# A two-block transformer step on one core: opening blocks merged, a layer norm folded into the next products, gates and last norm in parts, key choice in more steps

## What is computed

```python
# sparse attention: which keys each query may see
idx_s = relu(einsum('bqhd,bsd->bqhs', qib, ki))          # 8 index heads
idx_s = einsum('bqh,bqhs->bqs', wib, idx_s)
_, sel = top_k(where(causal, idx_s, -inf), 64)
# differential attention
lam = exp(sum(lp[0] * lp[1])) - exp(sum(lp[2] * lp[3])) + lam_init
# end of the first block, start of the second
x = rms_norm(x, final_norm_g)
h = x; hn = rmsnorm(h, attn_norm[0]); proj = hn @ w_in
# end of each layer
e = rmsnorm(p[i] @ ple_w_proj[i], ple_norm[i])
gate = sigmoid(rmsnorm(h, ple_gate_norm[i]) @ ple_w_gate[i])
h = h + gate * e
# end
return rmsnorm(h, final_norm)
```

## Time and profile before

| | |
|---|---|
| median of 3 runs | 2309.53 us (2305.46 to 2318.35) |
| the profiled execution | 2314.81 us, of which the span from first to last instruction 2313.0 |
| busy: TensorE / its weight loads | 1997.3 us (86%) / 1917.7 us (83%) |
| busy: DVE / ACT | 1529.7 us (66%) / 1222.2 us (53%) |
| granted TensorE clock, mean | 0.928 of full |
| HBM read | 293.26 MB, 127 GB/s over the span |

### The profile page before, as it was taken

The page is one execution under the profiler, slowest core; times in us unless marked ns, Lnnn a source line. Parts: engine busy times, 40 slices in busy tenths (PEclk is TensorE's granted clock), DMA queues, the critical chain, the costliest instruction groups (busy, mean ns, idle before and its releaser), DMA issues. The chain is left out here.

```text
span 2313.0 us, 44158 instructions
## 1 busy us (share of the span) xinstructions
PE 1997.3 (86%) x15796; PEld 1917.7 (83%) x15796; DVE 1529.7 (66%) x3122; ACT 1222.2 (53%) x2396; POOL 15.3 (1%) x21
## 2 busy tenths in 40 slices
PE   6998888999999766999999873896998968799895
PEld 5887778999999756999998863796998957799895
DVE  4657555999644688666665657765687567568755
ACT  4454554777755698555555453102555543555553
POOL 0000000000000000000000000000000001000000
PEclk9999998999999899999999996886999989799998
DMA  4422333445555301555554430001455523045441
GB/s 169 146 100 92 121 99 119 157 171 187 175 190 183 98 0 36 191 193 193 194 191 163 140 107 19 1 1 46 160 193 164 173 73 128 10 159 192 164 165 55
DMA packets 95216, 295.97 MB, mean 128 GB/s; under 512 B 9203, under 2 KB 25718, under 8 KB 94582
## 3 DMA queue, kind: packets, MB, share of 16 engines
q1 hardware_dynamic: 95094, 294.35, 37.9%
HBM read 293.26 MB, written 1.05 MB: 127 GB/s over the span
## 5 line engine op out<-in xcount | busy, mean ns | idle before, releaser
L381 PE MATMUL bank<-a_high,w_high 128*128 128x256 f32 x3256 | 937.9, 288 | 132.2 <-DVE a_low L741 61.9
L355 DVE TENSOR_TENSOR w_low<-ring,w_high 128x512 fp32r<-128x512 f32 x1102 | 747.3, 689 | 429.3 <-ACT w_high L349 424.5
L349 ACT ACTIVATE w_high<-ring 128x512 fp32r<-128x512 f32 x1102 | 680.0, 628 | 463.6 <-PE bank L383 459.6
L382 PE MATMUL bank<-a_low,w_high 128*128 128x256 f32 x3256 | 922.4, 283 | 0.0
L383 PE MATMUL bank<-a_high,w_low 128*128 128x256 f32 x3256 | 921.8, 283 | 0.0
L381 PEld LDWEIGHTS bank<-a_high,w_high 128*128 128x128 f32 x3256 | 632.9, 194 | 150.2 <-issue 107.1
L382 PEld LDWEIGHTS bank<-a_low,w_high 128*128 128x128 f32 x3256 | 629.4, 193 | 0.4
L383 PEld LDWEIGHTS bank<-a_high,w_low 128*128 128x128 f32 x3256 | 629.7, 193 | 0.0
L381 PE MATMUL bank<-s_high,w_high 128*128 128x256 f32 x1024 | 282.7, 276 | 2.0 <-DVE s_low L1872 2.0
L383 PE MATMUL bank<-s_high,w_low 128*128 128x256 f32 x1024 | 282.6, 276 | 0.0
L382 PE MATMUL bank<-s_low,w_high 128*128 128x256 f32 x1024 | 282.6, 276 | 0.0
(11 more groups left out here) (309 smaller groups left out, 2033.4 us busy)
## 6 DMA issues: line engine op xcount, KB each, us to landing
ring<-in_stream SPq DMA_DIRECT2D x279, 512.0 KB, 3.6
ring<-in_peer_u SPq DMA_DIRECT2D x128, 512.0 KB, 3.5
ring<-in_peer_v SPq DMA_DIRECT2D x128, 512.0 KB, 3.4
ring<-in_stream SPq DMA_DIRECT2D x32, 256.0 KB, 3.2
consts<-in_consts SPq DMA_DIRECT2D x1, 1024.0 KB
x<-in_x SPq DMA_DIRECT2D x1, 1024.0 KB, 7.1
arena<-in_mem SPq DMA_DIRECT2D x1, 1024.0 KB, 9.1
out<-x SPq DMA_DIRECT2D x1, 1024.0 KB, 4.0
```

What stands on the lines that cost most here:

```text
L349: self.nc.scalar.activation(self.w_high[:, h % SLOTS, :], self.raw(h), ACT.Copy)\
L355: self.nc.vector.tensor_tensor(self.w_low[:, h % SLOTS, :], self.raw(h), self.w_high[:, h % SLOTS, :].bitcast(F32), ALU.subtract)\
L381: self.nc.tensor.matmul(to, lh, rh, start=start, stop=False, **more)
L382: self.nc.tensor.matmul(to, lh, rl, start=False, stop=False, **more)
```

## The change

Five edits. (1) `load` issues lambda's row, six of the sixteen constants, x in four parts with a semaphore each, two weight groups, the other constants, two weight groups and the memory input, 14 DMAs, and waits for positions, params, lambda and the six constants; input copies and squares wait for their part of x. `lambda_of` is gone; its work is in `rope_tables`, with Exp ahead of Sin on ACT. (2) `choose_steps` scores two index heads a step in steps 0 to 7, with one Relu for both, and DVE does two multiply-adds a step; the maxima of a round come in an even step from 10 on, its replacements in the odd step after. (3) `between` is gone. The hybrid products take x times both gains (their product is made in `rope_tables`); with s the mean square of x and t the mean square of gained x, the root is over (s + eps) times (t/(s + eps) + eps). Squares of gained x go to an unused place, their sums to bank 6, and `whole` writes x times the first gain and root. (4) In `ple` the second block is gone; scaling e (`embed`), sigmoid and multiply-add (`apply`, by halves of a unit) are duties. (5) `finish` is one block with squares, gains on ACT, products and stores by pairs of chunks, and a small Sqrt first, which loads the table.

```diff
     def products(...)
+        if applied(len(units) - 1):
+            duties += [(units[norms[1][2]].end + 4, 4, "embed", c) for c in range(DC)]
...
-                    duties.append((max(end(u, h) + late, soon), 3, "unit", (u, h)))
+                    key = max(end(u, h) + late, soon)
+                    duties.append((key, 3, "unit", (u, h)))
+                    if applied(u):
+                        key = max(key, units[norms[1][2]].end + 4)
+                        duties += [(key + 1, 4, "sigmoid", (u, h)), (key + 2, 4, "apply", (u, h))]
...
# TensorE, sums of squares
+                            for c in range(norm.chunks if isinstance(norm, Twice) else 0):
+                                nc.tensor.matmul(self.bank[6][:, 0:T], self.const("ones"),
+                                                 norm.squares[:, c, :], start=c == 0,
+                                                 stop=c == norm.chunks - 1)
...
# ACT, squares and root
+                        if isinstance(norm, Twice):
+                            for c in range(norm.chunks):
+                                nc.scalar.activation(norm.squares[:, c, :], norm.source[:, c, :],
+                                                     ACT.Square, scale=self.param(norm.first, c))
...
+                        if isinstance(norms[what][0], Twice):
+                            nc.scalar.activation(inverse[1], inverse[1], ACT.Sqrt)
...
# DVE, root
+                        if isinstance(norms[what][0], Twice):
+                            link(nc.vector.tensor_scalar(inverse[1], summed[what], 1.0 / D, EPS,
+                                                         ALU.mult, ALU.add))
+                            link(nc.vector.reciprocal(inverse[1], inverse[1]))
+                            link(nc.vector.scalar_tensor_tensor(
+                                out=inverse[0], in0=self.bank[6][:, 0:T], scalar=1.0 / D,
+                                in1=inverse[1], op0=ALU.mult, op1=ALU.mult))
+                            link(nc.vector.tensor_scalar(inverse[0], inverse[0], EPS, None, ALU.add))
+                            link(nc.vector.reciprocal(inverse[0], inverse[0]))
+                            nc.vector.tensor_tensor(inverse[0], inverse[0], inverse[1], ALU.mult)\
+                                .then_inc(mean.up(), 1)
...
# DVE, the gates
+                    elif kind == "apply":
+                        u, h = what
+                        n = units[u].tile + 2 * h
+                        place, to = units[u].place, half(u, h)[1]
...
+                        link(nc.vector.tensor_tensor(to, to, place.by[:, n:n + 2, :], ALU.mult))
+                        nc.vector.tensor_tensor(place.to[:, n:n + 2, :], place.to[:, n:n + 2, :], to,
+                                                ALU.add)
...
     def load
-                for to, n in ((self.params[:, :], "params"), (self.consts[:, :, :], "consts")):
-                    sp.dma_start(to, self.dram[n]).then_inc(loaded.up(16), 16)
-                sp.dma_start(self.x[:, :, :], self.dram["x"]).then_inc(self.x_landed.up(16), 16)
+                sp.dma_start(self.consts[:, 0:soon, :], self.dram["consts"][:, 0:soon, :])\
+                    .then_inc(loaded.up(16), 16)
+                for c in range(4):
+                    sp.dma_start(self.x[:, 2 * c:2 * c + 2, :], self.dram["x"][:, 2 * c:2 * c + 2, :])\
+                        .then_inc(self.x_landed[c], 16)
...
     def choose_steps
-                if 18 <= i < 18 + N_SEL // 8:
+                if i in range(10, 10 + 2 * (N_SEL // 8), 2):
                     for b in range(TT):
                         ins = nc.vector.max(out=best[:, 8 * b:8 * b + 8], in_=total(b))
                     link(ins)
+                if i in range(11, 11 + 2 * (N_SEL // 8), 2):
                     for b in range(TT):
                         ins = nc.vector.match_replace(out=total(b), in_to_replace=best[:, 8 * b:8 * b + 8],
                                                       in_values=total(b), imm_value=TAKEN)
...
     def hybrid
-        h = Normed(x, "attn_norm_2.0")
+        h = Twice(x, "final_norm_g", "attn_norm_2.0", place(8))
+        free[0] -= 8 * T
...
     def finish
+                nc.scalar.activation(self.small[:, T:T + 1], self.const("ones")[:, 0:1], ACT.Sqrt)
+                for c in range(0, DC, 2):
+                    nc.scalar.activation(hn[:, c:c + 2, :], x[:, c:c + 2, :], ACT.Square)\
+                        .then_inc(squares.up(), 1)
...
+                for c in range(0, DC, 2):
+                    dve.wait_ge(gained.sem, gained.at(c + 2))
+                    nc.vector.tensor_tensor(x[:, c:c + 2, :], x[:, c:c + 2, :], inverse.unsqueeze(1)
+                                            .broadcast_to([P, 2, T]), ALU.mult).then_inc(ready.up(), 1)
...
+                for c in range(0, DC, 2):
+                    sp.wait_ge(ready.sem, ready.at(c // 2 + 1))
+                    sp.dma_start(self.out[:, c:c + 2, :], x[:, c:c + 2, :]).then_inc(stored.up(16), 16)
```

More of the change, by code:

```diff
@@ L136, with __init__ @@
 class Normed:
-    def __init__(self, source, gain, chunks=DC, size=D):
+    def __init__(self, source, gain, chunks=DC, size=D, ready=()):
         self.source, self.gain, self.chunks, self.size = source, gain, chunks, size
+        self.ready = ready
+class Twice(Normed):
+    def __init__(self, source, first, both, squares):
+        super().__init__(source, both)
+        self.first, self.squares = first, squares
 class Times:
@@ L921, in rope_tables @@
         MAGIC = 1.5 * 2.0 ** 23
+        dots, weights, exps = (self.counter(s) for s in ("lambda_dots", "lambda_spread", "lambda_exps"))
+        if lam is not None:
+            lambdas = self.at(70 * T, 1, 256)[0:1, 0, :]
+            prod = self.at(70 * T + 256, 1, 256)[0:1, 0, :]
+            dot = self.at(70 * T + 512, 1, 16)[0:1, 0, :]
         two_pi = 2 * math.pi
@@ L964, in _ @@
                                  start=True, stop=True).then_inc(spread.up(), 1)
+                if lam is not None:
+                    pe.wait_ge(dots.sem, dots.at(1))
+                    nc.tensor.matmul(self.bank[1][:, 0:2], self.consts[0:1, CONST_AT["ones"], :],
+                                     dot[:, 0:2], start=True, stop=True).then_inc(weights.up(), 1)
             @block.scalar
             def _(act):
+                if lam is not None:
+                    act.wait_ge(weights.sem, weights.at(1))
+                    nc.scalar.activation(lam[:, 1:3], self.bank[1][:, 0:2], ACT.Exp)\
+                        .then_inc(exps.up(), 1)
                 act.wait_ge(angles.sem, angles.at(1))
@@ L1349, in choose_steps @@
         count = 27
[L1350 to L1351 removed]
+        pairs = [(0, 2), (4, 6), (1, 3), (5, 7)] * 2
+        keys = lambda f: (f // 4 + 1) * P
+        part = lambda f: idx[:, 2 + 2 * (f % 2):4 + 2 * (f % 2), 0:keys(f)]
+        scores = lambda f: self.bank[bank][:, 0:2 * keys(f)].rearrange("p (h s) -> p h s", h=2)
         total = lambda b: idx[:, b, 0:(b + 1) * P]
@@ L1896, in expert_sum @@
         self.taken += N_KEYS * BLK
-    def between(self):
-        x = self.x
-        self.norm(lambda c: x[:, c, :], lambda c: self.param("final_norm_g", c),
-                  lambda c: x[:, c, :])
     def ffn(self, l):
@@ L1924, in ple @@
                        (f"ple_gate.{l}", "fm", Normed(x, f"ple_gate_norm_2.{l}"),
[L1925 to L1943 removed]
+                        Applied(lambda n, c: gate[:, n:n + c, :], e, f"ple_norm_2.{l}", x))],
+                      also=Normed(e, f"ple_norm_2.{l}"), after=(self.fetched, self.fetched.total))
     def mla(self):
@@ L2578, in finish @@
         nc = self.nc
-        x = self.x
-        self.norm(lambda c: x[:, c, :], lambda c: self.param("final_norm_2", c),
-                  lambda c: x[:, c, :])
-        stored = self.counter("stored")
-        with nc.Block(no_gpsimd_drain=True) as block:
+        x, hn = self.x, self.hn
+        squares, sums, mean, root, gained, ready, stored = (
+            self.counter(s) for s in ("squares_ready", "square_sums_ready", "mean_ready", "root_ready",
+                                     "gained", "output_ready", "stored"))
```

218 lines of the change are left out of this document (122 added, 96 removed).

## The result

The changed kernel takes 2294.61 us (median of 7 runs, 2289.82 to 2300.44), the kernel before in the same comparison 2312.89 (2300.59 to 2318.35): a ratio of 0.9927, 95% interval 0.9900 to 0.9953. That is 18.3 us less, and within 1.4 us of the forecast of 2293.2. The profiled execution of after has a span of 2298.5 us (it took 2300.44) at a mean granted clock of 0.926; before, 2313.0 at 0.928.

The account below looks back on a forecast made before the run. TensorE, busy 86%, bounds the kernel, so other engines' work matters only where it stands still. Start -3.0, choice -4.3, hybrid -4.8, gates -3.1 and end -1.1 sum to -16.3 us: 2293.2 us, range 2280 to 2305.

Parts of the forecast that it names:

- The start: Kernel start: lambda block removed, -3.7, against longer DMA issuing, net +0.7; sum -3.0 us, bounds -4 and -1.
- Rival 4: Kernel start: slow issues and a late exponent leave no gain there; total -13.3 us, 2296.2; chance 0.1.
- The key choice: Key choice: rounds spread over steps 10 to 25 take 5.7 us off DVE's late steps; -4.3, bounds -6 and 0.
- the deduction of 1.4 us: Key choice: 1.4 of the 5.7 us falls where DVE waits for TensorE's mixed values and a high weight part.
- rival 5: Key choice: paired scores make TensorE wait for ACT's Relu; at 3.6 us a step +12.5, 2322; chance 0.04.
- The hybrid: Hybrid products: folding in the final norm removes a block but lengthens the root; -4.8 us, bounds -8 and 0.
- three terms: Hybrid products: earlier start -11.5 us, eight more matmuls with ones +3.3, longer root chain on DVE and ACT +3.4.
- rival 2: Hybrid root and gates: new TensorE waits lower its clock, 10.8 us lost over three places; total -5.5, 2304; chance 0.12.
- The gates: Embedding gates: DVE work mostly changes places; layer 0 -0.5, layer 1 -2.6, sum -3.1 us, bounds -6 and +2.
- The end: Last norm and stores: 17.5 us after x is complete against 18.66; -1.1 us, bounds -3 and +1.5.
- Rival 3: Kernel end: ACT's table switch also drains, costing 1.4 us more; total -14.9, 2294.6; chance 0.06.
- Rival 1: DVE already full where work goes: gates 0, choice 2, hybrid start 3; total -8 us, 2301.5; chance 0.2.

Follow-up runs that it names:

- `only_choice`: The kernel before with the new key choice alone: 2302.08 us against 2309.96, ratio 0.9954.
- `only_hybrid`: The kernel before with the final norm folded into the hybrid products alone: 2307.82 us, ratio 1.0010 to before.
- `after_again`: The changed kernel, unedited, run and profiled a second time: 2294.48 us against 2313.53 before, ratio 0.9923.
- `one_sum`: The changed kernel without the hybrid norm's eight gained sums, second reciprocal and its small operations; trace only: shift against before -16.14 us at cut 690.
- `later_again`: The changed kernel with every norm's root two half-groups later, in a second comparison: 2279.17 us, ratio 0.9847 to before.
- `scale_one`: The changed kernel without seven of the eight embedding scalings in each gate; trace only: gates give -3.6 and -5.2 us against before.
- `only_ends`: The kernel before with the merged first blocks and the new `finish` alone: 2305.48 us, ratio 0.9978 to before.
- `old_root_later`: The kernel before with only every norm's root two half-groups later: 2291.20 us, ratio 0.9925 to before.
- `root_later`: The changed kernel with every norm's root two half-groups later, first comparison: 2267.12 us against 2304.87, ratio 0.9843.
- `both_later`: The changed kernel with every norm's root two half-groups later and the gained squares spread over weight cuts: 2275.74 us, ratio 0.9857 to before.
- `squares_spread`: The changed kernel with the eight gained squares spread over the first unit's weight cuts; trace only: hybrid stage gives -5.35 us to cut 690.

## Why the prediction was right

**The start: right at -3.0, with two sizes off.** The load block ended 1.25 us later, not 0.7. The wait of 1.4 us for constants went whole, as reckoned; the issues took longer, and end at 7.80, not 7.35: 2.64 us later than before. The first product gained only 2.5; the other 0.5 came by cut 10. Rival 4 (nothing at the start) falls.

**The key choice: mechanism right, size too small.** The step that failed is the deduction of 1.4 us: I took DVE's load in steps 18 to 25 as 5.7 less and said that 1.4 of it fell where DVE waits for TensorE's mixed values at 176. Alone it gives 6.5, all of the 5.7 and 0.8 more. The operation that takes the mixed values, before and in `only_choice`:

```profile
176.03 0.23 DVE L1114 TENSOR_SCALAR arena<-arena 128x4 f32<-128x4 f32 x1 [0.88 <-PE bank L1060]
```

```profile
174.19 0.23 DVE L1114 TENSOR_SCALAR arena<-arena 128x4 f32<-128x4 f32 x1 [1.68 <-PE bank L1060]
```

DVE's wait grows by 0.8 us, not 1.4, and the values do not stay at 176: against cut 50 they come 1.5 us earlier. Behind them stood seven of the eight rounds, now three pairs of maxima and four of replacements, 3.5 rounds or 5.0 us less. 1.5 + 5.0 = 6.5. What brings the mixed values forward was not tried by itself. The steps that took the moved work (scores from 125 to 168 us before) did not take it at no cost all along: in `only_choice` the shift against cut 50 is +3.7 at cut 62, and 0 again at cut 67. As it comes back within the stage, the forecast holds, and rival 5 (paired scores that wait) falls.

The clock is not what the choice gains by. In `only_hybrid`, with the old choice, it was at 1.00 from 165 to 206 us, TensorE waited 11.0 us for low weights instead of 8.5, and cuts 50 to 78 took only 0.25 us less than before; and the new choice gives 6.3 in `after_again` at 1.00, and 6.5 in after at 0.83. In all of them DVE's queue sets the end of the stage. Behind it the clock does count. In the first trace of after 0.8 us of the choice's gain were lost again by cut 82, with a fall at 193.4 us (0.83 on 190 to 200), and 1.5 more with a fall at 220.7 us (0.86 on 217 to 229); `after_again`, with 1.00 on both, lost nothing.

**The hybrid: three terms right, one missing.** -11.5 was -11.6, +3.3 and +3.4 were together +6.8 (of which `one_sum` gives back 6.0). Missing was the clock: behind the wait of 4.6 us it falls to 1.2 GHz, and the next half-groups lose 1.4 (after) to 2.8 us (`only_hybrid`). The windows behind the root, first after, then `after_again`:

```profile
1285.00:1292.00 7.00, 5.90 (x39) 5.90 (x40) 5.91 (x11) 3.19 (x7) 0.00 (x0) 0.76 0.47 150
```

```profile
1285.00:1295.00 10.00, 8.76 (x53) 8.76 (x54) 7.68 (x14) 4.15 (x8) 0.00 (x0) 0.66 0.37 123
```

So rival 2 came true in one of its three places, at under its size for one (3.6). In the gates the clock fell too, in one of the two traces each (layer 0: 0.83 on 1852 to 1862 in after, 1.00 in `after_again`; layer 1: 1.00 on 2270 to 2279 in after, 0.83 on 2268 to 2278 in `after_again`), but it cost nothing that shows: each gate's gain is the same in both to 0.1 us, since DVE ends it. The argument against the rival was the row with the wait of 1.26, which does not speak for a wait of 4.6. In `one_sum`, with waits of 2.0, the clock stayed at 1.00; in `later_again`, behind 2.55, it was 0.83 over 1280 to 1290. The length of the wait alone doesn't decide it: a wait of 3.1 us in the key choice of `only_hybrid`, at 190.7, left the clock at 1.00. The Trainium skill (TensorE: Matmul & The Clock Gate, HAM oscillation) says that idle gaps between matmuls bring the clock down: the trace agrees behind the gap of 4.6, and shows no fall behind those of 1.26 and 2.0.

**The gates: right, both a little larger.** -1.2 and -2.9 for -0.5 and -2.6. The DVE order was as I followed it, with TensorE waiting 1.9 and 0.8 us in layer 1 (forecast 1.9 and 1.3). That most of the work only changes places, and so a gate of eight scalings and two sweeps gives so little, is what `scale_one` shows: take DVE work away and nearly all of it comes back.

**The end: -1.8 to -2.6 for -1.1.** The mis-sized term is the eight sums. I took 6.73 us as they were; they took 6.25 (after), 5.40 (`after_again`) and 5.48 (`only_ends`), and the clock over them was 0.59, 0.68 and 0.67; before it was 0.59 too, so the 0.5 us between before and after stay open. What stands before and behind them took what I had reckoned to within 0.5. Rival 3 falls: ACT's load takes 1.28 us at 2282.00 and Sqrt follows at 2283.29, so a switch costs its load alone. The Trainium skill (ScalarE: Activation LUTs, What ACT_TABLE_LOAD costs) has 1.38 us of drain besides; the trace has none here, where ACT had been idle for 1.78 us, nor before at 421.29, where a load of 1.28 starts 0.02 us behind ACT's last operation and the next starts at 422.58.

**What cancelled.** Choice, gates and end gave 2.2 + 1.0 + 0.7 more than forecast in the first trace, the hybrid 1.4 less, and 4.4 went in unchanged stages. The forecast of the sum is good by that too. That the time was met within 1.4 us is luck besides: the forecast starts from a median of three runs, 3.4 us under that of seven, and the gain itself is 18.3 us, not 16.3. Rival 1, half the gain, falls on its own numbers (choice 2, gates 0).

## What to carry to other kernels

Where two engines prepare a third one's operands in a fixed order, ask of each operation that waits for the third (here a norm's root) what is queued behind it: two half-groups more of prepared weights ahead of it, one changed number, were worth as much as this whole change. When work on the critical path is cut, count also the clock: a new wait that is several times longer than those that the trace shows may cost more than its length (here 4.6 us, and 1.4 to 2.8 behind it). And compare two traces by a counted operation that both have, not by the span: here it separated six terms of 1 to 7 us in runs that spread by 10 to 20.

## What the runs showed that was not expected

**The same stage at two paces.** Between cuts 225 and 440, in the first layer's peer experts, no edit touches anything, and yet the shift moves: by -3.6 us in after, -5.7 in `old_root_later`, -5.5 in `root_later`, -3.8 to -7.2 in five others, and by -0.1 in `after_again`, -0.5 in `later_again` and +0.7 to +0.9 in `one_sum`, `both_later` and `only_ends`. As after and `after_again` are the same kernel, this belongs to the execution. The mean time from cut to cut has two values there, in all fourteen traces. From cut 300 to 350 it is 1.339 us in after, `root_later` and `old_root_later`, and 1.394 in before, `after_again`, `later_again` and `one_sum`, at a granted clock of 1.00. About the same stretch by window, in after and then in `after_again`:

```profile
612.00:674.00 62.00, 62.00 (x549) 62.00 (x548) 31.96 (x48) 40.53 (x74) 0.00 (x0) 1.00 0.60 198
```

```profile
607.00:672.00 65.00, 65.00 (x554) 65.00 (x554) 32.34 (x48) 40.86 (x74) 0.00 (x0) 1.00 0.56 188
```

TensorE waits for nothing in either; the matmuls themselves take 62.0/549 = 113 ns or 65.0/554 = 117 ns. The cause is open. Over these cuts two traces differ by up to 8 us. Of the 13 us between the spans of `root_later` and `later_again` it makes 5.0; 7.5 lie before cut 180. The ratios of the two to before, 0.9843 and 0.9847, do not differ.

**A long wait costs more than its length.** 4.6 us of waiting brought another 1.4, 2.7 and 2.8 us in after, `after_again` and `only_hybrid` (2.2 and 2.5 in `squares_spread` and `scale_one`), by a clock at its lower level. From the windows above it was there for 2 x (1 - 0.76) x 7 = 3.4 us in after and 2 x (1 - 0.66) x 10 = 6.8 in `after_again`.
